# Low halves of queries and values on VectorE in the attention of a decoder step, and one weight half moved ahead of two key halves

## The chip, the cores and the metric

The kernel runs on one core of a Trainium2 chip. The metric is device time in microseconds (us) of one execution, as a median of runs. The core has TensorE (matmuls), VectorE and ScalarE (elementwise work and reductions, from and to PSUM as well), GpSimd (elementwise work from SBUF) and SyncE (SP), which here issues every DMA. The engines run side by side and wait for one another through semaphores; each does its own instructions in the order in which they are written.

## The reference, cut to what matters

One decoder layer for 1024 prompt tokens and 8 sample tokens, all in float32: a gated recurrence and a pooling mixer, then cross-attention over 256 memory tokens with 4 heads of 256, then a SwiGLU block. The part around the change is the cross-attention:

```python
def mem_kv(mem, g, w_kv):
    kv = rmsnorm(mem, g) @ w_kv
    k, v = jnp.split(kv, 2, axis=-1)
    ...

def cross_attend(h, mk, mv, w_q, w_o):
    q = (h @ w_q).reshape(B, L, X_HEADS, X_HEAD_DIM)
    s = jnp.einsum('blhd,bmhd->bhlm', q, mk) * (X_HEAD_DIM ** -0.5)
    p = jax.nn.softmax(s, axis=-1)
    o = jnp.einsum('bhlm,bmhd->blhd', p, mv)
    return o.reshape(B, L, D_MODEL) @ w_o
```

Keys and values of the memory (new_mem_k, new_mem_v) are outputs as well. The sample tokens attend to cached keys and values of their own, 8 samples with 256 memory tokens each.

## The kernel before

**Halves.** Every float32 product is made of three matmuls in the float32r format: an operand is split into a high half (rounded by ScalarE) and a low half (the operand minus its high half, one `tensor_tensor` subtraction), and hi x hi, lo x hi and hi x lo are added in PSUM. So each stripe of weights, and each block of queries, keys, values and softmax weights, costs a rounding on ScalarE and a subtraction on VectorE or GpSimd before TensorE may use it.

**Phases.** The phases run one after the other; the change lies in `kv` (keys and values of the memory) and in the attention behind it. In `kv` TensorE runs 8 key stripes and 8 value stripes, stripes 0 to 15; value stripe n is stripe 8 + n. Between them it computes the scores of the 8 samples (`sample_scores`), scores(0) and scores(1) of the prompt, and the first turn of softmax weights. The prompt's queries come in 8 blocks of 128 tokens (PAIRS = 8, numbered 0 to 7).

**TensorE's order** (the inner functions of `keys_values` and `attention` of the TensorE block): stripes 8, 9, sample 4, stripes 10, 11, sample 5, stripe 12, scores(0), stripe 13, sample 6, scores(1), turn_p(0), sample 7, stripe 14. Then for n = 1 to 7: scores(n + 1), turn_p(n) (transposes of block n's softmax weights), at n = 1 the last value stripe, from n = 3 on one or two `sample_values`, and from n = 2 on values(n - 2). scores(n) waits for the exponentials of n - 1 (they read the same PSUM banks) and for `qs_made`, the low half of query block n. turn_p(n) waits for `turned_rest(n - 1)`.

**Who makes what.** ScalarE: rounding of weight stripes (`w_hi`), of query blocks (`q_block`, tile `qs`, two buffers), of keys (`k_hi`), of values (`value_round`, tile `v_hi`), and four exponentials per block (`exps`). VectorE: the low halves of weight stripes (`split_low`, L1912), of keys (`key_rest`, L1935), the maximum (`maxima`, L1917), the normalisation (`normalize`, L1922 and L1924), the low half of turned weights (`turned_rest`, L1972), of outputs (`output_rest`, L1996), and the plain values (`value_kept`, L1966). GpSimd: the low halves of queries (`query_rest`, L928) and of values (`value_rest`, L936, in two halves of columns), masks, and the masked weights of the samples (L959).

**Stores that other work waits for.** The low half of the keys overwrites kT, so `key_rest` waits until the store of kT (L735) has landed; the low half of the values overwrites vnat, so `value_rest` waits for the store of that half of mem_v (L713).

**SP's order in `kv`.** For i = 3 to 7: loads of the two stripes 2i and 2i + 1 (each waits until the stripe whose buffer it takes has its low half), for i = 6 the store of kT (waits until all of kT is evacuated), then the cached keys of sample i - 1. Behind the loop come the keys of sample 7, the first mem_v store, loads of the next phase and of cached values, and the second mem_v store.

Of the kernel before, what the change touches and what calls it, by code (L numbers as in the profile page):

```python
# [29 lines left out]
F32 = mybir.dt.float32  # L30
# [4 lines left out]
P = 128  # L35
# [53 lines left out]
def hybrid_layer(nc, t):  # L89
# [9 lines left out]
    with ExitStack() as ctx:  # L99
# [421 lines left out]
        def _(sp):  # L521
            def load_stripe(p, i, s, wait=True):
                v, off, step, extra = stripe_src(p, i, s)
                if wait:

                    if p.name == "kv":
                        sp.wait_ge(lo_made, p.first + 2 * KV_FREE[i] + s + 1)
                    else:
                        sp.wait_ge(lo_made, p.first + 2 * i + s - 1)
                kb = v.shape[1]  # L530
                if p.name == "kv" and i >= KP:
                    dst, arrived, _ = raw_slot(p, i, s)
                    sp.dma_start(dst.rearrange("p (k a) c -> p k (a c)", k=2), v).then_inc(arrived, 16)
                    return
                src = v[:, :, bass.ds(i * step + (off + extra), P)]
                if p.name == "kv":
                    dst, arrived, _ = raw_slot(p, i, s)
                    sp.dma_start(dst, src).then_inc(arrived, 16)
                else:
                    sp.dma_start(raw[:, s, 0:kb, :], src).then_inc(raw_in[s], 16)  # L540
# [98 lines left out]
            for p in phases:  # L639
# [85 lines left out]
                if p.name == "kv":  # L725
                    sp.wait_ge(mem_step, 6)
                    sp.wait_ge(mem_sq, 2)
                    for s in range(2):
                        load_keys(1, s)
                    for i in range(3, p.stripes // 2):  # L730
                        for s in range(2):
                            load_stripe(p, i, s)
                        if i == 6:
                            sp.wait_ge(evac, p.done + KB)
                            sp.dma_start(t["mem_k_cols"], kT[:, :, :]).then_inc(kn_out, 16)  # L735
                        for s in range(2):
                            load_keys(i - 1, s)
                    for s in range(2):
                        load_keys(7, s)
# [60 lines left out]
        def _(pool):  # L800
# [124 lines left out]
            def query_rest(n):  # L925

                pool.wait_ge(q_round, QR + n + 1)
                pool.tensor_tensor(o_lo[:, :, n * P:(n + 1) * P], qT[:, :, n * P:(n + 1) * P], qs[n % 2][:, :, :].bitcast(F32),  # L928
                                   ALU.subtract).then_inc(qs_made, 1)

            def value_rest(c):

                pool.wait_ge(v_out, VO + 16 * (c + 1))
                pool.wait_ge(v_round, VR + 2 * (c + 1))
                at = slice(c * 512, (c + 1) * 512)
                pool.tensor_tensor(v_lo[:, :, at], vnat[:, :, at], v_hi[c][:, :, :].bitcast(F32), ALU.subtract).then_inc(v_rest, 1)  # L936

            def sample_values():

                for n in range(2):  # L940
                    query_rest(n)
                value_rest(0)
                for n in range(2, 4):
                    query_rest(n)
                pool.wait_ge(sk_done, NS + 1)
                pool.memset(smask[:, :, :], 0.0).then_inc(smask_made, 1)
                pool.wait_ge(smask_made, 1)
                for b in range(NS):
                    last = pool.memset(smask[:, b, b * H:(b + 1) * H], 1.0)
                last.then_inc(smask_made, 1)  # L950
                value_rest(1)
                query_rest(4)

                pool.wait_ge(ssm, 4)
                pool.wait_ge(smask_made, 2)
                for n in range(NS):
                    if n >= 2:
                        pool.wait_ge(sv_done, 2 * n - 2)
                    pool.tensor_tensor(spz[n % 2], spT[:, :, :], smask[:, n:n + 1, :].to_broadcast([P, 2, NS * H]),  # L959
                                       ALU.mult).then_inc(spz_made, 1)  # L960
                    if 1 <= n <= 3:
                        query_rest(n + 4)

            def squares(p, i, s, c):
                e = 6 * i + 3 * s + c
# [570 lines left out]
        def _(dve):  # L1536
# [369 lines left out]
            def split_low(m):  # L1906

                n = (p, m // 2, m % 2) if m < 16 else (ph["co"], 0, m - 16)
                count = n[0].first + 2 * n[1] + n[2]
                dve.wait_ge(lo_made, count)  # L1910
                dve.wait_ge(hi_made, count + 1)
                dve.tensor_tensor(w_lo[n[2]][:, :, :], raw_slot(*n)[0], w_hi[n[2]][:, :, :].bitcast(F32),  # L1912
                                  ALU.subtract).then_inc(lo_made, 1)
# [13 lines left out]
            def keys_values(p):  # L1927
                def turned_evac(j):
                    dve.wait_ge(mm_done, p.done + j + 1)
                    dve.tensor_tensor(kT[:, j, :], bank[4 + j % 2][:, 0:M], rbm[:, :], ALU.mult).then_inc(evac, 1)  # L1930

                def key_rest(n):
                    dve.wait_ge(kn_out, 16)
                    dve.wait_ge(k_round, KR + n + 1)
                    dve.scalar_tensor_tensor(k_lo[:, 4 * n:4 * n + 4, :], kT[:, 4 * n:4 * n + 4, :], -SCALE,  # L1935
                                             k_hi[:, 4 * n:4 * n + 4, :].bitcast(F32), ALU.mult,
                                             ALU.subtract).then_inc(k_rest, 1)

                split_low(1)
                for j in range(KB):  # L1940
                    turned_evac(j)
                    split_low(j + 2)
                split_low(10)
                key_rest(0)
                split_low(11)
                key_rest(1)
                split_low(12)
                value_kept(0, 0)
                value_kept(0, 1)
                split_low(13)  # L1950
                split_low(14)
                maxima(0)
                normalize(0)
                split_low(15)
                maxima(1)
                sample_maxima()
                normalize(1)
                sample_normalize()
                turned_rest(0)
                split_low(16)  # L1960

            def value_kept(c, a):
                dve.wait_ge(v_round, VR + 2 * c + a + 1)
# [11 lines left out]
            def sample_maxima():  # L1975
                dve.wait_ge(sk_done, NS + 1)
                dve.tensor_reduce(sst[:, 0:1], bank[7][:, 0:M], AX_X, ALU.min).then_inc(ssm, 1)
# [14 lines left out]
            def attention():  # L1992
                def output_rest(u):
                    dve.wait_ge(pv_hi, u + 1)
                    rows, at = slice(4 * (u % 2), 4 * (u % 2) + 4), slice(u // 2 * M, (u // 2 + 1) * M)
                    dve.tensor_tensor(o_lo[:, rows, at], wide(V_BANKS[u]).rearrange("p (k c) -> p k c", k=4),  # L1996
                                      o_hi[:, rows, at].bitcast(F32), ALU.subtract).then_inc(pv_out, 1)

                for n in range(1, PAIRS):
                    if n + 1 < PAIRS:  # L2000
                        maxima(n + 1)
                        normalize(n + 1)
                    if n == 2:
                        sample_turned()
                    turned_rest(n)
                    if n == 1:
                        value_kept(1, 0)
                        value_kept(1, 1)
                        split_low(17)
                    if n >= 2:  # L2010
                        output_rest(n - 2)
                output_rest(6)
                output_rest(7)

                dve.wait_ge(so_turned, 1)
                turned = [bank[6 + h // 2][:, 0:P].rearrange("p (k b h) -> p k b h", k=4, h=H)[:, 2 * (h % 2):2 * (h % 2) + 2, :, h]
                          for h in range(H)]
                for h in range(H):
                    last = dve.tensor_copy(o_hi[:, 2 * h:2 * h + 2, TP:T], turned[h])
                last.then_inc(so_made, 1)  # L2020
                dve.wait_ge(so_made, 1)
                for h in range(H):
                    last = dve.tensor_tensor(o_lo[:, 2 * h:2 * h + 2, TP:T], turned[h],
                                             o_hi[:, 2 * h:2 * h + 2, TP:T].bitcast(F32), ALU.subtract)
                last.then_inc(so_made, 1)
# [756 lines left out]
```

## Time and profile before

| what | value |
|---|---|
| median of 3 runs | 1440.44 us (1439.74 to 1442.37) |
| the profiled execution's own time | 1440.8 us |
| its span in the trace | 1439.1 us |
| mean granted TensorE clock | 0.994 of full speed |
| TensorE busy | 1409.3 us, 98% of the span |
| VectorE busy | 883.9 us, 61% |
| ScalarE busy | 420.3 us, 29% |
| GpSimd busy | 595.0 us, 41% |

All times of a row are microseconds from the start of the span. In the profile PE is TensorE, DVE is VectorE, ACT is ScalarE, POOL is GpSimd, and SPq is SP's queue of DMA issues. A busy share says how much an engine works, not whether somebody waits for it. So the reader goes from the engine table to the list of waits, and from there to the instructions in order of time around each wait: a row ends with the idle time ahead of it in brackets and the instruction that ended it. TensorE's matmul rows overlap by some 0.1 us, so the end of a group is best read from the start of the next.

### The profile page before, as it was taken

The page shows a single profiled execution, that of the slowest core. Times are in us where ns is not written, and L with a number is a line of the kernel's source. Part 1 is how long each engine was busy: PE and PEld are TensorE (multiplying, and loading weights), DVE is VectorE, ACT ScalarE, POOL GpSimd, SP SyncE. Part 2 cuts the span into 40 slices and gives each one's busy share as a digit, 9 for nine tenths or more (in the row PEclk, how much of TensorE's full clock was granted, in tenths as well). Part 3 has the DMA queues.
Part 4 walks back from the last instruction along what each step waited for, and adds up shares of the span by engine and source line. Part 5 has one row for each costly group of instructions (what it writes and reads, how often), then busy time and mean ns, then how long its engine had stood idle before and what let it go on. Part 6 is the DMA issues. An engine that isn't in the chain of part 4 may idle for free.

```text
span 1439.1 us, 25488 instructions
## 1 busy us (share of the span) xinstructions
PE 1409.3 (98%) x9965; PEld 1367.0 (95%) x9965; DVE 883.9 (61%) x1343; ACT 420.3 (29%) x632; POOL 595.0 (41%) x464
## 2 busy tenths in 40 slices
PE   8999999999999999899999999999999999999997
PEld 7999999989999977799999999999999999999996
DVE  4425677778753346557996666776677658632335
ACT  6131344471021135420052323232323223311111
POOL 1241246045532002424563877787777710000163
PEclk9999999999999999999999999999999999999998
DMA  9412111101161274511122222222222142523113
GB/s 294 125 44 79 54 30 38 38 23 59 44 190 44 87 259 140 184 63 45 44 74 79 84 88 73 71 75 88 73 80 66 59 143 85 169 89 113 34 44 118
DMA packets 163567, 129.19 MB, mean 90 GB/s; under 512 B 11532, under 2 KB 148748, under 8 KB 163363
## 3 DMA queue, kind: packets, MB, share of 16 engines
q1 hardware_dynamic: 163499, 128.25, 28.7%
q8 instruction: 47, 0.77, 0.2%
q14 instruction: 21, 0.17, 0.0%
HBM read 107.88 MB, written 20.58 MB: 89 GB/s over the span
## 4 chain that ended last, share of the span: by engine, by line
PE 62%; POOL 14%; issue 11%; DVE 7%; ACT 2%; DMA 1%; SPq 1%; POOLq 0%; DVEq 0%; ACTq 0%
PE pm L2235 17%; PE pm L2237 17%; PE pm L2236 17%; POOL gb L1003 3%; POOL raw_c L985 3%; POOL raw L985 3%; POOL sum L992 2%; POOL sum L990 2%; PE pm L2506 1%; PE pm L2508 1%; PE pm L2507 1%; DMA xt<-in_x_prompt 1%; POOL raw L997 1%; POOL raw_c L997 1%; DVE w_lo L1549 1%
## 5 line engine op out<-in xcount | busy, mean ns | idle before, releaser
L2235 PE MATMUL pm<-x_hi,w_hi 128*128 128x344 f32 x960 | 310.5, 323 | 0.7 <-DVE gb L1616 0.7
L2237 PE MATMUL pm<-x_hi,w_lo 128*128 128x344 f32 x960 | 306.6, 319 | 0.0
L2236 PE MATMUL pm<-x_lo,w_hi 128*128 128x344 f32 x960 | 306.6, 319 | 0.0
L1088 ACT ACTIVATE w_hi<-raw 128x1024 fp32r<-128x1024 f32 x88 | 93.4, 1061 | 530.3 <-PE pm L2237 465.4
L2235 PEld LDWEIGHTS pm<-x_hi,w_hi 128*128 128x128 f32 x960 | 180.4, 188 | 2.6 <-issue 1.9
L2236 PEld LDWEIGHTS pm<-x_lo,w_hi 128*128 128x128 f32 x960 | 180.4, 188 | 0.2
L2237 PEld LDWEIGHTS pm<-x_hi,w_lo 128*128 128x128 f32 x960 | 180.4, 188 | 0.0
L1549 DVE TENSOR_TENSOR w_lo<-raw,w_hi 128x1024 fp32r<-128x1024 f32 x79 | 113.8, 1440 | 10.0 <-ACT w_hi L1088 10.0
L831 POOL TENSOR_TENSOR raw<-raw,gains 128x1024 f32<-128x1024 f32 x32 | 64.7, 2026 | 127.3 <-DMA raw<-in_w_in 81.1
L2082 DVE TENSOR_TENSOR gb<-gb,ga 128x1032 f32<-128x1032 f32 x19 | 53.0, 2788 | 89.9 <-POOL gb L1003 89.9
L913 POOL TENSOR_TENSOR fp<-acc 128x344 f32 (+1 forms) x22 | 21.3, 969 | 201.8 <-DVE acc L2193 196.9
L2193 DVE TENSOR_TENSOR acc<-pm,acc 128x344 f32<-128x344 f32 x66 | 33.9, 516 | 112.1 <-PE pm L2237 112.0
L1002 POOL TENSOR_TENSOR ga<-ga,rb 128x1032 f32<-128x1032 f32 x19 | 52.6, 2768 | 85.9 <-DVE ga L2098 85.9
L2506 PE MATMUL pm<-x_hi,w_hi 128*128 128x258 f32 x304 | 86.5, 285 | 0.2
L2507 PE MATMUL pm<-tl,wh 128*128 128x258 f32 x304 | 85.9, 283 | 0.0
L2506 PE MATMUL pm<-th,wh 128*128 128x258 f32 x304 | 85.9, 282 | 0.0
L2508 PE MATMUL pm<-th,wl 128*128 128x258 f32 x304 | 85.9, 282 | 0.0
L2507 PE MATMUL pm<-tl,w_hi 128*128 128x258 f32 x304 | 85.8, 282 | 0.0
L2508 PE MATMUL pm<-x_hi,w_lo 128*128 128x258 f32 x304 | 85.8, 282 | 0.0
L2508 PE MATMUL pm<-th,w_lo 128*128 128x258 f32 x304 | 85.7, 282 | 0.0
L2507 PE MATMUL pm<-x_lo,w_hi 128*128 128x258 f32 x304 | 85.7, 282 | 0.0
L2506 PE MATMUL pm<-th,w_hi 128*128 128x258 f32 x304 | 85.7, 282 | 0.0
(364 smaller groups left out, 3996.2 us busy)
## 6 DMA issues: line engine op xcount, KB each, us to landing
raw<-in_w_ffn_in SPq DMA_DIRECT2D x24, 512.0 KB, 4.5
sg_raw<-s_rows SPq DMA_DIRECT2D x22, 516.0 KB, 5.1
s_rows<-gb SPq DMA_DIRECT2D x21, 516.0 KB, 2.7
raw<-in_w_in SPq DMA_DIRECT2D x20, 512.0 KB, 3.8
raw_c<-in_w_ffn_in SPq DMA_DIRECT2D x20, 512.0 KB, 5.0
sk<-in_cache_k_cols SPq DMA_DIRECT2D x16, 512.0 KB, 6.4
raw<-in_w_out SPq DMA_DIRECT2D x8, 512.0 KB, 3.6
raw<-in_w_cq SPq DMA_DIRECT2D x8, 512.0 KB, 3.5
```

Source lines behind the costliest of these rows:

```text
L831: pool.tensor_tensor(raw[:, s, :, :], raw[:, s, :, :], g, ALU.mult).then_inc(gain_on, 1)
L985: pool.tensor_tensor(r[:, s, :, :], r[:, s, :, :], g, ALU.mult).then_inc(gain7_on, 1)
L1002: pool.tensor_tensor(ga[:, :], ga[:, :], rb[:, :], ALU.mult).then_inc(row_scaled, 1)
L1088: act.activation(w_hi[s][:, :, :], src, ACT.Copy).then_inc(hi_made, 1)
L1549: dve.tensor_tensor(w_lo[s][:, :, :], raw[:, s, :, :], w_hi[s][:, :, :].bitcast(F32), ALU.subtract).then_inc(lo_made, 1)
L2082: dve.tensor_tensor(gb[par][:, :], gb[par][:, :], ga[:, :], ALU.mult).then_inc(row_made, 1)
L2235: pe.matmul(out, w_hi[s][:, k, :], hi[:, k, x0:x0 + cols], start=(k == 0), stop=False)
L2236: pe.matmul(out, w_hi[s][:, k, :], lo[:, k, x0:x0 + cols], start=False, stop=False)
L2237: last = pe.matmul(out, w_lo[s][:, k, :], hi[:, k, x0:x0 + cols], start=False, stop=(k == kb - 1))
L2506: pe.matmul(out, wh7[n][:, j, :], hi(j, c), start=j == 0, stop=False)
L2507: pe.matmul(out, wh7[n][:, j, :], lo(j, c), start=False, stop=False)
L2508: last = pe.matmul(out, wl7[n][:, j, :], hi(j, c), start=False, stop=j == KP - 1)
```

## The change

- VectorE gets `query_rest` and `value_rest`. The low halves of query blocks 2 to 7 and of the first half of the values are made there; GpSimd keeps those of blocks 0 and 1 and of the second half of the values, which also waits for the first.
- In VectorE's queue query_rest(n) stands between a maximum and the normalisation behind it: block 2 between maxima(0) and normalize(0), 3 between maxima(1) and normalize(1), and 4 to 7 between maxima and normalize of blocks 3 to 6. value_rest(0) stands behind split_low(15) and ahead of maxima(1).
- split_low(11) goes ahead of key_rest(0) and split_low(12) ahead of key_rest(1).
- In SP's queue the store of kT goes ahead of the loads of stripes 12 and 13.

```diff
@@ SP, phase kv
                     for i in range(3, p.stripes // 2):
-                        for s in range(2):
-                            load_stripe(p, i, s)
                         if i == 6:
                             sp.wait_ge(evac, p.done + KB)
                             sp.dma_start(t["mem_k_cols"], kT[:, :, :]).then_inc(kn_out, 16)
+                        for s in range(2):
+                            load_stripe(p, i, s)
                         for s in range(2):
                             load_keys(i - 1, s)
@@ GpSimd
                 pool.wait_ge(v_round, VR + 2 * (c + 1))
+                pool.wait_ge(v_rest, VL + 1)
@@ GpSimd, sample_values
                 for n in range(2):
-                    query_rest(n)
-                value_rest(0)
-                for n in range(2, 4):
                     query_rest(n)
@@
                 value_rest(1)
-                query_rest(4)
@@
-                    if 1 <= n <= 3:
-                        query_rest(n + 4)
@@ VectorE, keys_values
                 split_low(10)
+                split_low(11)
                 key_rest(0)
-                split_low(11)
+                split_low(12)
                 key_rest(1)
-                split_low(12)
                 value_kept(0, 0)
                 value_kept(0, 1)
                 split_low(13)
                 split_low(14)
                 maxima(0)
+                query_rest(2)
                 normalize(0)
                 split_low(15)
+                value_rest(0)
                 maxima(1)
                 sample_maxima()
+                query_rest(3)
                 normalize(1)
@@ VectorE, new functions
+            def query_rest(n):
+                dve.wait_ge(q_round, QR + n + 1)
+                dve.wait_ge(qs_made, n)
+                dve.tensor_tensor(o_lo[:, :, n * P:(n + 1) * P], qT[:, :, n * P:(n + 1) * P], qs[n % 2][:, :, :].bitcast(F32),
+                                  ALU.subtract).then_inc(qs_made, 1)
+
+            def value_rest(c):
+                dve.wait_ge(v_out, VO + 16 * (c + 1))
+                dve.wait_ge(v_round, VR + 2 * (c + 1))
+                at = slice(c * 512, (c + 1) * 512)
+                dve.tensor_tensor(v_lo[:, :, at], vnat[:, :, at], v_hi[c][:, :, :].bitcast(F32), ALU.subtract).then_inc(v_rest, 1)
@@ VectorE, attention
                     if n + 1 < PAIRS:
                         maxima(n + 1)
+                        if n >= 2 and n + 2 < PAIRS:
+                            query_rest(n + 2)
                         normalize(n + 1)
```

## Rows read from the trace of the kernel before

**Rows 1.** The page's engine table: busy us, share of the span, instructions.
```profile
PE 1409.3 (98%) x9965; PEld 1367.0 (95%) x9965; DVE 883.9 (61%) x1343; ACT 420.3 (29%) x632; POOL 595.0 (41%) x464
```

**Rows 2.** TensorE's waits, whole span: us in total, times, longest us.
```profile
PE pm L2549 <- POOL o_lo L928: 6.1, 1, 6.1
...
PE pm L2608 <- DVE w_lo L1912: 2.5, 1, 2.5
PE pm L2549 <- ACT pr L1321: 1.7, 2, 1.5
```

**Rows 3.** Stretches: length, busy PE PEld DVE ACT POOL, granted clock, DMA share, GB/s.
```profile
534.00:536.00 2.00, 0.09 (x1) 0.00 (x0) 1.86 (x2) 1.06 (x1) 0.00 (x0) 1.00 0.96 381
538.00:539.00 1.00, 1.00 (x4) 0.73 (x3) 0.77 (x1) 0.25 (x1) 0.00 (x0) 0.50 0.51 137
580.00:581.00 1.00, 0.00 (x0) 0.00 (x0) 1.00 (x2) 0.00 (x0) 1.00 (x1) 0.50 0.00 0
620.00:700.00 80.00, 80.00 (x533) 79.75 (x532) 57.43 (x90) 10.52 (x11) 33.13 (x36) 1.00 0.16 47
```

**Rows 4.** TensorE in order of time: start, us, instruction, idle before.
```profile
536.56 0.50 PE L2608 MATMUL pm<-w_hi,m_hi 128*128 128x512 f32 x1 [2.47 <-DVE w_lo L1912]
...
561.12 0.36 PE L2549 MATMUL pm<-k_hi,qs 128*128 128x256 f32 x1 [1.47 <-ACT pr L1321]
564.19 1.06 PE L2560 MATMUL pm<-ident,pr 128*128 128x128 f32 x8
...
581.52 0.58 PE L2549 MATMUL pm<-k_hi,qs 128*128 128x256 f32 x1 [6.08 <-POOL o_lo L928]
```

**Rows 5.** The chain that ended last, in order of time: start, us, what.
```profile
530.14 0.98 PE pm L2574 x16
...
541.16 0.98 PE pm L2574 x16
...
586.29 0.87 PE pm L2560 x8
```

**Rows 6.** VectorE from 534 us on, in order of time.
```profile
534.14 1.22 DVE L1935 SCALAR_TENSOR_TENSOR k_lo<-kT,k_hi 128x1024 fp32r<-128x1024 f32 x1 [4.23 <-DMA out_mem_k_cols<-kT]
535.28 1.22 DVE L1912 TENSOR_TENSOR w_lo<-raw,w_hi 128x1024 fp32r<-128x1024 f32 x1
```

**Rows 7.** SP's queue: the kT store.
```profile
526.43 0.47 SPq L735 DMA_DIRECT2D out_mem_k_cols<-kT  x1
```

**Rows 8.** DMA issues at 526.4, 527.4, 543.0 and 572.2: KB, us to landing.
```profile
out_mem_k_cols<-kT SPq DMA_DIRECT2D x1, 1024.0 KB, 7.7
...
sk<-in_cache_k_cols SPq DMA_DIRECT2D x1, 512.0 KB, 9.2
...
out_mem_v<-vnat SPq DMA_DIRECT2D x1, 512.0 KB, 8.0
...
out_mem_v<-vnat SPq DMA_DIRECT2D x1, 512.0 KB, 3.5
```

**Rows 9.** GpSimd in order of time, 551 to 582 us.
```profile
553.43 6.70 POOL L928 TENSOR_TENSOR o_lo<-qT,qs 128x1024 fp32r<-128x1024 f32 x2
...
575.83 2.35 POOL L936 TENSOR_TENSOR v_lo<-vnat,v_hi 128x1024 fp32r<-128x1024 f32 x1 [15.07 <-DMA out_mem_v<-vnat]
578.13 3.34 POOL L928 TENSOR_TENSOR o_lo<-qT,qs 128x1024 fp32r<-128x1024 f32 x1
```

**Rows 10.** VectorE in the attention, in order of time.
```profile
576.70 0.18 DVE L1922 RECIPROCAL rden<-den 128x4 f32<-128x4 f32 x1 [2.00 <-ACT pr L1321]
576.92 2.33 DVE L1924 TENSOR_TENSOR pr<-pr,rden 128x1024 f32<-128x1024 f32 x1
...
594.09 1.23 DVE L1917 TENSOR_REDUCE nmax<-pm 128x4 f32<-128x1024 f32 x1 [0.57 <-PE pm L2551]
...
602.73 1.22 DVE L1917 TENSOR_REDUCE nmax<-pm 128x4 f32<-128x1024 f32 x1 [0.57 <-PE pm L2551]
```

**Rows 11.** ScalarE: the last query rounding.
```profile
600.80 1.06 ACT L1314 ACTIVATE qs<-qT 128x1024 fp32r<-128x1024 f32 x1
```

## The prediction, made before the changed kernel was run

> **What bounds the kernel now.** I read the engine table first, then TensorE's waits, then the stretches. TensorE is busy 98% of the span and no other engine passes 61% [rows 1]: what the kernel can gain is what TensorE stands idle, plus what it runs at the lower clock. The table of TensorE's waits says where it stands [rows 2]: 6.1 us for the queries' low halves of GpSimd (one wait), 2.5 us for a weight half of VectorE (one wait), 1.7 us in two waits for the exponentials. All lie between 534 and 582 us, where keys and values end and the attention begins. Behind the attention the stretch from 620 to 700 us has 80.00 busy us of 80.00 [rows 3], so what is won ahead of it is kept.
>
> The clock is the second loss. The granted clock is 0.50 (1.2 GHz) in the samples behind the 2.5 us wait and behind the 6.1 us wait [rows 3]; before both it was 1.00. In durations: a value stripe takes 531.12 to 534.09, 2.97 us, and the one behind the first wait 536.56 to 541.16, 4.60 us: 1.6 us lost. The scores of a pair take 561.12 to 564.19, 3.07 us, and those behind the second wait 581.52 to 586.29, 4.77 us: 1.7 us lost [rows 4, 5]. The wait of 1.47 us at 561.12 was followed by full speed (the same 3.07 us).
>
> So the pot is 2.5 + 1.6 + 1.5 + 0.2 + 6.1 + 1.7 = 13.6 us of a profiled run of 1440.8 us.
>
> **Part 1: SP's order and the order of three VectorE instructions.** Value stripe 3 (stripe 11) starts at 536.56, when its low half, made 535.28 to 536.50, is there. That half stood in VectorE's queue behind k_lo (L1935), which had waited 4.23 us for the store of kT to land and began at 534.14 [rows 4, 6]. Now split_low(11) stands ahead of key_rest(0). ScalarE rounds it when stripe 9 is done, at 530.1 [rows 5], in 1.06 us (a row of the same size) [rows 11], so it can be made by about 532.5, ahead of 534.09 where TensorE wants it. The 2.5 us wait goes, and the clock's 1.6 us with it. No instruction is added.
>
> What is late next: key_rest(0), then split_low(12). TensorE wants stripe 12's low half at 538.0 (stripe 3 and one sample product of 0.98 us later), and ScalarE rounds it at 534.2 to 535.2 in either order, so split_low(12) ends at 536.5 if key_rest(0) has begun by 534.0. It needs the kT store. SP issued this at 526.43, right behind stripe 13's load [rows 7]; now it goes as soon as kT is whole, about 524.0, and by the 7.7 us of its row [rows 8] it lands at 531.7; it would have to be 2.3 us later to cost anything. The two raw_b loads are moved behind it: stripe 12's by about 1.4 us (at the 7.7 us of the store it lands at 532.2, wanted at 534.1), stripe 13's not at all, since it waited for a VectorE half until 526.0. Cost: nothing, from the slack of 2 us; if that is gone, the wait comes back a stripe later.
>
> The keys of sample 5 follow, and TensorE now wants them 4.1 us earlier. Their second half landed 9.2 us after its issue at about 527.4, so at 536.6 [rows 8]; the sample product is now due at 537.1. Same bytes ahead of them, so the same landing: 0 us, with 0.5 us of slack only. Bounds: 0 and 1.5 us, since the DMA engines are 0.96 busy from 534 to 536 [rows 3] and can't catch up. I take 0.
>
> **Part 2: the low halves on VectorE.** Removed from GpSimd: six query_rest and one value_rest. They took 2.4 to 3.4 us each: two in 6.70 us at 553.43, one of 3.34 us at 578.13 [rows 9]. Added to VectorE: seven tensor_tensor of the same 128x1024 size. Beside an idle GpSimd VectorE does such an instruction in 1.22 us (the halves at 534.14 and 535.28) [rows 6]. That is 8.5 us more on an engine with gaps.
>
> Where they lie: between maxima(n) and normalize(n) VectorE waits 2.00 us for ScalarE's four exponentials, in every step (576.70 is one of seven such rows; the wait at 561.00 is 1.67) [rows 10]. One instruction of 1.14 to 1.22 us fits, if its rounded query is there. The last of them was made at 600.80 to 601.86, and the maximum in whose shadow it is now used began at 602.73 [rows 10, 11]: there ahead of time. Cost: 0; uncovered it would be 6 x 1.2 = 7.3 us.
>
> What goes: (a) GpSimd's chain. At 575.83 it began v_lo of the second half (it had waited 15.07 us, in the end for the mem_v store), with query 4's low half behind it, which ended at 581.47: TensorE's 6.1 us [rows 9]. Now that half is in VectorE's queue, at about 569. (b) Mutual blocking. The 1.22 us normalisation took 2.33 at 576.92, ending 1.07 us after GpSimd's v_lo ended at 578.18, and GpSimd's row behind it took 3.34 where others took 2.4 [rows 9, 10]. It stretched VectorE's work behind 551 us, beside GpSimd's 6.70 us, in the same way. Without it maxima(1) isn't late, and the 1.5 us wait of scores(2) goes.
>
> What is late next. With every wait gone TensorE would be ready for scores(4) at 581.5 - 2.5 - 1.6 - 1.5 - 0.2 - 6.1 = 569.6. It then needs exponentials 3. Before, these ended at 576.6, when TensorE had been free since 575.44: 1.2 us that the GpSimd wait covered [rows 5, 10]. VectorE is now less behind at maxima(2) (0.3 instead of 0.9 us), so I take 0.7 us; bounds 0 and 1.4.
>
> One GpSimd instruction of size is left: v_lo of the second half. Its store took 3.5 us [rows 8]. It goes when both vnat halves are written, when SP issued it at 572.2 [rows 8]; TensorE's stripe 7 ahead of them comes 2.5 + 1.6 + 1.5 = 5.6 us earlier, ScalarE's exponentials 2 another 0.6: 566.0. So GpSimd works 569.6 to 572.0. normalize(3), due at 570.5, is held to 572.0, as the row of 2.33 us shows [rows 10], and ends at 573.1; sample_turned (0.3) and turned_rest(2) (1.2) let turn_p(3) start at 574.5. TensorE, with scores(4) from 570.3, is done at 573.4: 1.1 us (bounds 0 and 2.0, the second if v_lo starts 1 us later).
>
> The Trainium skill (Perfetto Trace Analysis, Optimizing Scalar/DVE Operations) speaks against this part: the two engines share an SBUF read port, so offloading between them "might not help". The rows do show the blocking, but also 1.22 us for the work on one engine and 2.4 on the other; by the skill's rule the sum would be that of rival 2.
>
> **An added wait.** value_rest(0) stands in VectorE's queue for the first mem_v store, and behind it maxima(1), exponentials 1 and scores(2). The store took 8.0 us [rows 8]. It is now issued at about 539.1 (4 us earlier), so it lands at 547.1. VectorE reaches it at 549.8 and maxima(1) is due at 550.6: 0 us; it would cost from a landing after 551.2 on (exponentials 1 have that slack).
>
> **Sum.** 13.6 us, minus 0.7, minus 1.1: 11.8 us. From the profiled run's 1440.8 us this gives 1429.0; the median of the runs shown, 1440.44, is 0.4 us lower, so the forecast is 1428.6.
>
> **Rivals.**
> 1. *A transfer takes the wait's place.* Keys 5 late, or the kT store landing after 534, or the mem_v store after 551.2. For it: DMA share 0.96 around 535 [rows 3]. Against: each has slack by the rows. Price: one wait of about 2.5 us with its low clock, 2.5 + 1.6 = 4.1, leaves a gain of 7.7: 1432.7, and up to 1434. Chance 0.14.
> 2. *The move buys nothing*: the port is held by VectorE instead, the exponentials and halves keep TensorE waiting as long as GpSimd did. Then only part 1 (4.1 us) stays: 1436.3. Against: GpSimd's 3.34 us instructions become 1.22 us. Chance 0.04.
> 3. *Part 1 does not do what it says* (the half of stripe 11 is late for another reason, its load), part 2 works: 11.8 - 4.1 = 7.7, again 1432.7. Chance 0.04.
> 4. *Slower: VectorE becomes the bound of the attention.* A step on it is the maximum (1.2), 2.0 us of exponentials with the new instruction inside, and three more of 1.22 with a reciprocal (3.9): 7.1 us, against 8.6 us from maximum to maximum as TensorE sets them now (594.09 to 602.73) [rows 10]. It decides when the step passes 8.6: not with one blocked instruction, but if the remaining GpSimd products held both two-input instructions of a step for 3.3 us, as VectorE held GpSimd's at 578.13 [rows 9]. Then a step is 1.2 + 3.3 + 3.3 + 2.4 + 0.2 = 10.4 us; five steps lose 1.8 each and, with a gap in each, 1.7 of clock: 17.5 us, less the 11.8: 1446.1. Against: VectorE still waits for TensorE before each maximum from 594 on (0.57 us at 594.09 and 602.73) [rows 10]. Chance 0.03.
>
> **How the numbers follow.** The forecast has 0.75. Its own range: all bounds good, 13.6 us gained, 1426.8; all bad (0.7 + 0.9 + 1.5 more lost), 1431.7. To hold 8 in 10 I reach into rivals 1 and 3: 1426.0 to 1433.5. A measurement of this kernel tells 0.2%, 2.9 us. Faster by more: 0.75 + 0.14 + 0.04 + 0.04 less a little of each that is worse than priced: 0.94. Within: 0.03. Slower: 0.03.
>
> **What would show it.** Right: no TensorE wait at L2608 and stripe 3 next to stripe 2; clock 1.00 from 530 to 620; scores(4) starts near 570 us after a wait under 1.5 us on exponentials; query halves of 1.2 us inside the 2 us of the exponentials; one GpSimd v_lo with a stretched normalisation beside it. Wrong: a new wait of TensorE on sample keys (L2574) or on L1935, VectorE idle before value_rest(0), or low clock anywhere in the stretch.

## The result, and the profile after

| | before | after |
|---|---|---|
| median of the runs side by side | 1441.35 us (4 runs) | 1429.83 us (4 runs) |
| profiled execution's own time | 1440.8 us | 1430.4 us |
| its span | 1439.1 us | 1428.7 us |
| mean granted TensorE clock | 0.994 | 0.997 |

The ratio of the times is 0.9928, with a 95% interval of 0.9915 to 0.994: 0.7% faster, which is 10.4 us (8.6 to 12.3). The two medians of the table differ by 11.5 us; the ratio and its interval are what the document goes by. The forecast was 1428.6 us, 11.8 us less than the 1440.44 known then, in a range of 1426.0 to 1433.5.

TensorE's waits after, in the same view as [rows 2] (us in total, times, longest). Of the three rows of before, the GpSimd one (6.1 us) and the weight half (2.5 us) are gone; a wait for exponentials of 1.4 us is left, a new one of 0.9 us stands at turn_p, and one of 0.5 us at the keys of a sample.

```profile
PE pm L2561 <- ACT pr L1316: 1.4, 1, 1.4
...
PE pm L2572 <- DVE o_lo L1982: 0.9, 1, 0.9
...
PE pm L2586 <- DMA sk<-in_cache_k_cols: 0.5, 1, 0.5
```

The stretches after, as in [rows 3]: the granted clock is 1.00 over the whole attention, and the stretch behind it is as full as before.

```profile
530.00:620.00 90.00, 87.06 (x672) 72.21 (x671) 63.61 (x66) 48.06 (x101) 6.96 (x18) 1.00 0.55 189
...
620.00:700.00 80.00, 80.00 (x515) 79.75 (x515) 63.23 (x99) 7.43 (x7) 40.64 (x42) 1.00 0.13 39
```

VectorE after, in order of time, the same view as [rows 6, 10]. The reader is to see the half of stripe 11 at 532.43, ahead of the key half; the value half at 550.88 with no idle time ahead of it; and the query half of 1.21 us at 569.66 between the maximum and the reciprocal, which now waits 0.87 us for the exponentials where it waited 2.00.

```profile
532.43 1.23 DVE L1907 TENSOR_TENSOR w_lo<-raw,w_hi 128x1024 fp32r<-128x1024 f32 x1 [1.49 <-ACT w_hi L1083]
533.57 1.22 DVE L1930 SCALAR_TENSOR_TENSOR k_lo<-kT,k_hi 128x1024 fp32r<-128x1024 f32 x1
...
550.88 1.22 DVE L1970 TENSOR_TENSOR v_lo<-vnat,v_hi 128x1024 fp32r<-128x1024 f32 x1
552.02 1.22 DVE L1912 TENSOR_REDUCE nmax<-pm 128x4 f32<-128x1024 f32 x1
...
567.39 1.22 DVE L1907 TENSOR_TENSOR w_lo<-raw,w_hi 128x1024 fp32r<-128x1024 f32 x1
568.53 1.22 DVE L1912 TENSOR_REDUCE nmax<-pm 128x4 f32<-128x1024 f32 x1
569.66 1.21 DVE L1963 TENSOR_TENSOR o_lo<-qT,qs 128x1024 fp32r<-128x1024 f32 x1
571.75 0.18 DVE L1917 RECIPROCAL rden<-den 128x4 f32<-128x4 f32 x1 [0.87 <-ACT pr L1316]
571.96 2.40 DVE L1919 TENSOR_TENSOR pr<-pr,rden 128x1024 f32<-128x1024 f32 x1
```

The normalisation at 571.96 takes 2.40 us. GpSimd's row beside it, the one large instruction left there (compare [rows 9]), ran until 573.28:

```profile
570.90 2.38 POOL L937 TENSOR_TENSOR v_lo<-vnat,v_hi 128x1024 fp32r<-128x1024 f32 x1 [16.37 <-DMA out_mem_v<-vnat]
```

TensorE's two waits in order of time, as in [rows 4]: scores(4) at 571.86 (before 581.52), and turn_p(3) held by turned_rest(2) behind that normalisation.

```profile
571.86 0.35 PE L2561 MATMUL pm<-k_hi,qs 128*128 128x256 f32 x1 [1.40 <-ACT pr L1316]
...
575.84 1.07 PE L2572 MATMUL pm<-ident,pr 128*128 128x128 f32 x8 [0.91 <-DVE o_lo L1982]
```

The sum of the two traces closes. scores(4) starts 9.7 us earlier (581.52 to 571.86); its 24 matmuls take 3.1 us instead of 4.8, another 1.7; the new wait of 0.9 us is given back: 10.5 us, against 10.4 of the spans. But this is the sum of a larger gain and a loss. In a part that the change does not touch, at the spreading of the first norm factors, TensorE waited 0.22 us for ScalarE before and 1.44 us after:

```profile
35.70 0.90 PE L2255 MATMUL pm<-ident,rtok 128*128 128x128 f32 x6 [0.22 <-ACT rtok L1123]
```

```profile
36.76 0.90 PE L2267 MATMUL pm<-ident,rtok 128*128 128x128 f32 x6 [1.44 <-ACT rtok L1118]
```

So everything up to stripe 10 comes 1.0 us later: the product of sample 4 starts at 530.1 before and at 531.1 after. From there to turn_p(3) TensorE took 56.2 us before (to 586.3) and 44.7 after (to 575.8): the stretch that was changed is 11.5 us shorter.

### The profile page after: what moved, and what is told of

It is laid out like the page before. It is cut to its first block, busy times and chain, and to the rows that moved or that the text cites. A ratio compares the mean times of both kernels' runs of the same rounds, so it can differ in the third digit from the quotient of the medians.

```text
span 1428.7 us, 25494 instructions
## 1 busy us (share of the span) xinstructions
PE 1404.9 (98%) x9965; PEld 1364.1 (95%) x9965; DVE 886.8 (62%) x1350; ACT 420.3 (29%) x632; POOL 577.5 (40%) x457
## 4 chain that ended last, share of the span: by engine, by line
PE 65%; POOL 12%; issue 10%; DVE 7%; ACT 2%; DMA 2%; SPq 1%; POOLq 0%; DVEq 0%; ACTq 0%
PE pm L2247 17%; PE pm L2249 17%; PE pm L2248 17%; POOL gb L998 2%; POOL raw_c L980 2%; POOL raw L980 2%; PE pm L2518 2%; PE pm L2520 2%; PE pm L2519 2%; POOL sum L987 2%; POOL sum L985 2%; DMA xt<-in_x_prompt 1%; DMA sk<-in_cache_k_cols 1%; DVE w_lo L1544 1%; POOL raw L992 1%
```

## The experiments

The question: do the two parts of the change do what the prediction says, and do they add up? The rivals: the place in a queue and not the engine; the place of the store and not that of the halves; a pot that either part empties; and VectorE being full. There are twelve runs.

**The order alone** (SP's and VectorE's order changed; all low halves stay on GpSimd).

```diff
--- before
+++ this
@@ SP
-                        for s in range(2):
-                            load_stripe(p, i, s)
                         if i == 6:
...
+                        for s in range(2):
+                            load_stripe(p, i, s)
@@ VectorE
                 split_low(10)
+                split_low(11)
                 key_rest(0)
-                split_low(11)
+                split_low(12)
                 key_rest(1)
-                split_low(12)
```

> Only the order is changed (SP's kT store ahead of the loads of stripes 12 and 13, split_low(11) and split_low(12) one place ahead); the low halves stay on GpSimd. My theory: the two parts of the change add up, and this one is worth the 2.5 us wait of value stripe 3 and the 1.6 us of low clock behind it: 4.1 us, 1437 us. The waits of 1.5 us (scores of block 2) and 6.1 us (scores of block 4) and the low clock behind the latter stay. Rival 'one pot': what is won here is given back at the attention, because GpSimd's mem_v store sets its own time: then the 6.1 us wait grows to about 10 us and the time stays near 1441.

Measured: ratio 0.9965 [0.9953, 0.9976], 5.0 us faster; in its profile the wait and the low clock at stripe 3 are gone, and the attention is that of before, the 6.2 us wait included. The span is 4.3 us shorter than before's. The theory stands: nothing is given back.

```profile
PE pm L2549 <- POOL o_lo L928: 6.2, 1, 6.2
```

**The halves alone, twice** (the second time profiled beside before).

```diff
--- the change
+++ this (low halves as in the change, order as before)
@@ SP
+                        for s in range(2):
+                            load_stripe(p, i, s)
                         if i == 6:
...
-                        for s in range(2):
-                            load_stripe(p, i, s)
@@ VectorE
                 split_low(10)
-                split_low(11)
                 key_rest(0)
+                split_low(11)
-                split_low(12)
                 key_rest(1)
+                split_low(12)
```

> Only the low halves are moved to VectorE; SP's order and the order of the weight and key halves are those of before. My theory: 1.5 + 0.2 + 6.1 + 1.7 us go, 1.4 (exponentials of block 3) and 0.9 us (turn_p(3)) stay: 7.2 us won, 1434 us; the 2.5 us wait of stripe 3 and its low clock stay. Rival 'one pot': with stripe 3 late the chain behind it has more slack, and the whole 11 us minus less than 2 come from this part: 1431.

> The low halves alone on VectorE, the order as before, profiled once more beside before. Theory 'it varies with the landing': 1430.5 us again, a wait of stripe 3 anywhere from 0.5 to 2.5 us and equal to the landing of the kT store less about 5.2 us. Rival 'in this kernel the wait is short': 1.4 us again and no low clock, while before shows 2.5 us beside it.

> The kernel before itself, profiled once more. Open: the wait of value stripe 3 was 2.47 us with a low clock behind it in the first profile of before, and 1.39 us with none in the run of the halves alone, whose instructions up to there are the same. Theory 'it varies with the landing': the kT store lands 5 to 8 us after its issue from run to run, and the wait is that landing less about 5.2 us; the clock falls only when the wait is over 2 us. Then this run shows 0.5 to 2.5 us. Rival 'the first profile is typical': 2.4 to 2.5 us and 1.6 us of low clock again. The 6.1 us wait is there in either case: 1439 to 1441 us.

Measured: the halves alone have ratio 0.9929 [0.9913, 0.9946], and 0.994 [0.9922, 0.9958] the second time: 10.2 and 8.6 us faster, where 7.2 was expected. 1430.77 us is what the rival 'one pot' had named for the first, but not by its mechanism: the waits at scores(4) and turn_p(3) are those of the whole change, and no slack took them up. The whole change in its two sets of runs isn't clearly more, 0.9928 and 0.9926. The waits left in their profiles account for it: 13.6 - 1.4 - 1.4 - 0.9 = 9.9 us, and 13.6 - 2.5 - 1.4 - 1.1 = 8.6, if no clock is lost at stripe 3. So the parts don't add (5.0 + 9.4 = 14.4 against 10.5). Of the 3.9 us between, 1.6 are clock at stripe 3, which the order alone wins and the halves alone don't lose, up to 1.1 are the shorter wait in the first profile of the halves alone, and 0.5 the wait for keys in the profile of the change; the rest is within the intervals. TensorE at stripe 3 shows the first two. The rows of before again, of the halves alone and of the halves alone again:

```profile
537.89 0.66 PE L2608 MATMUL pm<-w_hi,m_hi 128*128 128x512 f32 x1 [2.09 <-DVE w_lo L1912]
```

```profile
535.03 0.50 PE L2620 MATMUL pm<-w_hi,m_hi 128*128 128x512 f32 x1 [1.39 <-DVE w_lo L1907]
```

```profile
536.24 0.50 PE L2620 MATMUL pm<-w_hi,m_hi 128*128 128x512 f32 x1 [2.48 <-DVE w_lo L1907]
```

The wait was 2.47 [rows 4] and 2.09 us in the two profiles of before and 1.39 and 2.48 us in the two of the halves alone. It follows the landing of the kT store, which came 7.7, 7.3, 6.6 and 7.7 us after its issue. Less 5.2 these are 2.5, 2.1, 1.4 and 2.5: that half of the theory holds. The other half, that the clock falls only behind a longer wait, falls: behind 2.09 us it fell, behind 2.48 us it didn't. First before again, then the halves alone again, the microseconds behind the wait (columns as in [rows 3]):

```profile
540.00:541.00 1.00, 1.00 (x4) 0.75 (x3) 0.10 (x1) 0.28 (x1) 0.00 (x0) 0.50 0.72 172
```

```profile
538.00:539.00 1.00, 1.00 (x6) 0.72 (x4) 0.74 (x2) 0.62 (x1) 0.00 (x0) 1.00 0.92 190
```

Both profiles of before had the 1.6 us of low clock at stripe 3, and both of the halves alone had not. Up to there the two kernels issue the same instructions, so I can't name a cause in the kernel, and two against two may be chance. This is left open; the time it decides is 1.6 us.

**The whole change without SP's move, and without VectorE's reordering.**

```diff
--- the change
+++ without SP's move
@@ SP
+                        for s in range(2):
+                            load_stripe(p, i, s)
                         if i == 6:
...
-                        for s in range(2):
-                            load_stripe(p, i, s)
--- the change
+++ without the reordering
@@ VectorE
-                split_low(11)
                 key_rest(0)
+                split_low(11)
-                split_low(12)
                 key_rest(1)
+                split_low(12)
```

> The whole change without SP's part: the kT store is issued behind the loads of stripes 12 and 13, as before. My theory: the order on VectorE alone is enough. The store lands at about 535 instead of 532.9, the first key half is made behind it and stripe 12's half by 537.6, due at 539: no wait, 1430 us, as the whole change. Rival 'the store's place carries it': stripe 12 now waits where stripe 3 waited, 2 us and a low clock, 1433.5 us.

> The whole change without VectorE's part of the order: split_low(11) stands behind key_rest(0) as before, the kT store is still moved ahead on SP. My theory: the store lands at 532.9, the key half takes until 534.1, stripe 11's half until 535.3, and TensorE wants it at 535.1: a wait of 0.3 us with no low clock behind it, 1430 us. Rival 'only the queue order matters': the wait is 1.5 us or more and the clock falls, 1433 us.

Measured: 1429.59 us, ratio 0.9923 [0.9906, 0.9939], and 1431.02 us, ratio 0.9932 [0.9909, 0.9954]. Neither has a wait at stripe 3 or stripe 12. Without SP's move the key half waits 1.17 us for the store, at 533.31, and harms nobody, since both weight halves come in time. Without the reordering the store landed early, 5.3 us after its issue at 524.96, and the key half at 530.80 was done before stripe 11's rounded half was there:

```profile
530.80 1.22 DVE L1930 SCALAR_TENSOR_TENSOR k_lo<-kT,k_hi 128x1024 fp32r<-128x1024 f32 x1
532.37 1.23 DVE L1907 TENSOR_TENSOR w_lo<-raw,w_hi 128x1024 fp32r<-128x1024 f32 x1 [0.35 <-ACT w_hi L1083]
```

In these runs either half of part 1 was enough, and neither rival ("the store's place carries it", "only the queue order matters") came. The second wasn't put to a hard test: at the 7.9 us of the change's own store a short wait was expected, and no run shows that case. The same store landed 5.1 to 7.9 us after its issue in all kernels but the one with three more edits below, so the order on VectorE is the sturdier of the two: it doesn't depend on a landing.

**All low halves on GpSimd, one swap in its queue.**

```diff
--- the order alone
+++ this
@@ GpSimd
-                value_rest(1)
                 query_rest(4)
+                value_rest(1)
```

> The order part of the change, and all low halves still on GpSimd, with one swap in its queue: query block 4's half ahead of the second v_lo (before: behind it). My theory: most of the 6.1 us wait came from that place in the queue. Scores of block 4 then wait only for the exponentials (1 to 2 us), the clock doesn't fall; the 1.5 us wait at scores(2) stays, since that comes from GpSimd and VectorE blocking each other. Won: 4.1 + 4.5 + 1.7 = about 10, less 1 to 2 us for blocked VectorE instructions: 1432 us. Rival 'the engine matters': GpSimd's 2.4 to 3.4 us instructions keep block 4 or the next blocks late, and it gives no more than the order alone, 1437 us.

Measured: 1432.07 us, ratio 0.9947 [0.9929, 0.9965], 7.6 us faster by the ratio; 1432 was expected. The 6.1 us wait for GpSimd is gone with the low halves still there: it came from the place of query 4 behind v_lo in GpSimd's queue. What is left is what the two engines do to each other. Its VectorE and GpSimd rows:

```profile
548.48 3.42 DVE L1912 TENSOR_TENSOR w_lo<-raw,w_hi 128x1024 fp32r<-128x1024 f32 x1
...
555.24 2.33 DVE L1924 TENSOR_TENSOR pr<-pr,rden 128x1024 f32<-128x1024 f32 x1
...
567.48 2.50 DVE L1912 TENSOR_TENSOR w_lo<-raw,w_hi 128x1024 fp32r<-128x1024 f32 x1
```

```profile
566.51 2.39 POOL L928 TENSOR_TENSOR o_lo<-qT,qs 128x1024 fp32r<-128x1024 f32 x1 [9.38 <-ACT qs L1314]
```

Three VectorE instructions of 1.22 us take 2.3 to 3.4. TensorE waits 1.1 us at turn_p(1), where a wait of 1.5 us at scores(2) was expected. At scores(4) it waits 2.7 us for exponentials whose maximum stood behind the 2.50 us one; the granted clock was 0.50 from 575 to 577, and this run of scores took 4.2 us instead of 3.1.

```profile
573.23 0.36 PE L2549 MATMUL pm<-k_hi,qs 128*128 128x256 f32 x1 [2.67 <-ACT pr L1321]
```

These rows lose 5.1 us (2.7 + 1.1 + 1.1 of clock + 0.2 at scores(3)), those of the change 2.3 to 2.8. So by the rows the move to VectorE is worth some 2 to 3 us beyond a mere reordering; the intervals of the two ratios, 0.9929 to 0.9965 and 0.9915 to 0.994, still overlap.

**The last large GpSimd instruction on VectorE.**

```diff
--- the change
+++ this
@@ GpSimd
-                value_rest(1)
@@ VectorE, attention
                     turned_rest(n)
+                    if n == 2:
+                        value_rest(1)
```

> The whole change, and the second half of the values' low half also on VectorE, behind turned_rest(2); GpSimd has no large instruction left. My theory: the normalisation of block 3 takes 1.22 instead of 2.40 us, turn_p(3) doesn't wait (0.9 us won), and the maximum of block 4 comes at the same time as before, since 1.2 us less blocking pays for 1.2 us more work: 1429 us. Rival 'VectorE is full': the maximum of block 4 is later and scores(5) waits for its exponentials, 1430 us or more.

Measured: 1428.04 us, ratio 0.992 [0.9902, 0.9938]. The normalisation of block 3 takes 1.23 us, the wait at turn_p(3) is gone, and no wait stands at scores(5). The maximum of block 4 starts 1.8 us after scores(4) ends in either kernel (575.21 and 573.44; in the change 576.75 and 574.93). As expected: VectorE isn't full.

**The weight half of the next phase behind the maximum.**

```diff
--- the change
+++ this
@@ VectorE, attention
                         maxima(n + 1)
+                        if n == 2:
+                            split_low(17)
...
                         value_kept(1, 1)
-                        split_low(17)
```

> The whole change, and split_low(17), the low half of a weight stripe that TensorE wants only after the attention, moved from ahead of the maximum of block 3 to behind it. My theory: the wait of scores(4) for the exponentials falls from 1.4 to about 0.3 us, but the normalisation of block 3 is still held by GpSimd's v_lo, so turn_p(3) starts at the same time and waits about 2.0 us instead of 0.9: nothing won, 1430 us. Rival 'the waits add': 1.1 us won, 1428.7 us.

> The changed kernel with split_low(17) behind the maximum of block 3, again and in more rounds: 1426.3 us, 2.3 us under the changed kernel (1428.7 to 1429.8). The normalisation of block 3 starts 0.1 us ahead of GpSimd's v_lo, which then waits for it. If that order is a matter of luck, this run shows the normalisation held for 1 us and a wait of turn_p(3) instead, and 1427.3 us.

Measured: 1426.2 us, ratio 0.9909 [0.9891, 0.9926], and 1429.19 us, ratio 0.9909 [0.9889, 0.9929], where the runs of before beside it were slower as well. My theory of no gain fell, and the rival was too small. The wait at scores(4) fell from 1.40 to 0.21 us as expected (it is now for the query's low half), but the one at turn_p(3) went as well. VectorE, then GpSimd, of the first of the two runs:

```profile
568.72 0.17 DVE L1917 RECIPROCAL rden<-den 128x4 f32<-128x4 f32 x1
568.93 1.22 DVE L1919 TENSOR_TENSOR pr<-pr,rden 128x1024 f32<-128x1024 f32 x1
```

```profile
569.05 3.38 POOL L937 TENSOR_TENSOR v_lo<-vnat,v_hi 128x1024 fp32r<-128x1024 f32 x1 [16.36 <-DMA out_mem_v<-vnat]
```

The normalisation started 0.12 us ahead of v_lo, took 1.22 us, and GpSimd took 3.38 instead of 2.38. In the change it started 1.06 us behind (571.96 and 570.90) and VectorE lost instead. In the repeated run the gap was 0.06 us (573.17 and 573.23), with the same outcome. This agrees with the Trainium skill (SBUF — State Buffer, Who interferes with whom): a VectorE instruction with two SBUF inputs contends with a GpSimd instruction that reads SBUF, and the order of issue decides which of them blocks. The 1 us is paid in either case; on GpSimd nobody waits for it.

**All three remaining waits at once, beside the change again.**

```diff
--- the change
+++ this (with both edits above as well)
@@ SP
-                        if i == 6:
-                            sp.wait_ge(evac, p.done + KB)
-                            sp.dma_start(t["mem_k_cols"], kT[:, :, :]).then_inc(kn_out, 16)
                         for s in range(2):
                             load_stripe(p, i, s)
                         for s in range(2):
                             load_keys(i - 1, s)
+                        if i == 6:
+                            sp.wait_ge(evac, p.done + KB)
+                            sp.dma_start(t["mem_k_cols"], kT[:, :, :]).then_inc(kn_out, 16)
@@ VectorE
                 split_low(11)
-                key_rest(0)
                 split_low(12)
+                key_rest(0)
                 key_rest(1)
```

> The whole change with three more edits: the second v_lo on VectorE, split_low(17) behind the maximum of block 3, and the keys of sample 5 ahead of the kT store in SP's queue with both key halves behind split_low(12). My theory: the waits left in the stretch (0.46 us for the keys of sample 5, 1.4 us at scores(4), 0.9 us at turn_p(3)) all go, with 0.2 us left at scores(5): 2.5 us won against the changed kernel beside it, 1427.3 us if that is 1429.8. Rival 'VectorE is full': the waits reappear at scores(5) or at scores(0), and less than 1 us is won.

> The changed kernel itself again, beside the run above on the same chip: 1429.8 us, waits of 0.46, 1.4 and 0.9 us in the stretch from 530 to 580 us.

Measured: 1426.93 us, ratio 0.9909 [0.9894, 0.9924], beside 1428.65 us, ratio 0.9926 [0.9913, 0.9939], of the change. So 1.7 us were won against the 2.5 expected. The kT store, now last, was issued at 527.5 and landed at 537.8, 10.3 us later; both key halves and the values behind them came late, and scores(0) waited 0.8 us. That is a place which the rival named, but for the store and not because VectorE is full:

```profile
537.85 2.36 DVE L1929 SCALAR_TENSOR_TENSOR k_lo<-kT,k_hi 128x1024 fp32r<-128x1024 f32 x2 [1.17 <-DMA out_mem_k_cols<-kT]
540.12 1.40 DVE L1975 TENSOR_SCALAR vnat<-pm,rtok 128x512 f32<-128x512 f32 x2
```

The change, profiled again, showed 1.40 and 0.90 us, nearly as in its first profile, but no wait for sample 5's keys, and no other profile has it: the 0.46 us is a matter of one run's landing, and the third edit mends nothing. The best ratio seen is 0.9909, twice with split_low(17) alone moved and once with all three edits, against 0.9928 and 0.9926 for the change. The intervals overlap, so the last 2 us or so rest on the profiles (1.40 to 0.21 and 0.91 to none) as much as on the times.

## Why the prediction was right, point by point

- **What bounds.** Right. TensorE's waits and the clock were the whole pot, and behind the attention nothing was given back (80.00 of 80.00 us from 620 to 700 both times).
- **Part 1, 4.1 us.** Right against before: the wait is gone in the profile, and the order alone measured 5.0. Stripe 12 and its load were in time. As a term of a sum it isn't shown: on top of part 2 the order brought about 1 us (10.5 against 9.4), which the intervals don't tell from nothing. That a single one of the two moves can suffice I had not said. The 1.6 us of clock in the term isn't tied to the wait alone: the halves alone kept a 2.48 us wait at full speed.
- **Keys of sample 5.** I took 0 us with bounds of 0 and 1.5. The trace has 0.46 us, and 0 in the change profiled again: the slack of 0.5 us was used up in one run. There the second half of the keys was issued at 528.66 and took 9.5 us, not 9.2.
- **Part 2, the wait of 6.1 us and the 1.5 us at scores(2).** Both gone, with the clock's 1.7. Of the two mechanisms named, the queue place (a) was the larger: GpSimd reordered has no wait for GpSimd either. The blocking (b) stretches the rows as said, but that the 1.5 us of scores(2) come from it alone isn't shown: with GpSimd reordered three rows are still stretched, and there the wait is 1.1 us at turn_p(1) and none at scores(2).
- **The added instructions cost nothing.** Right: 1.21 us each while VectorE waited for exponentials anyway, which left 0.87 of 2.00 us of idle time (none in block 1's step, where the sample's maximum stands there too); value_rest(0) found its store landed (no idle time ahead of 550.88), 7.4 us after its issue at 540.26.
- **Exponentials 3, 0.7 us.** Too small: 1.40, at my upper bound. The step that failed is "VectorE is now less behind at maxima(2) (0.3 instead of 0.9 us)". Measured from the start of scores(2), that maximum came 3.62 us later (556.52 to 560.14), against 3.97 before (561.12 to 565.09): only 0.35 us less. From maxima(2) to maxima(3) VectorE took 8.4 us in both. And TensorE's own way from scores(2) to the end of values(0) was 13.94 us, against 14.32 before with a wait of 0.2 in it, which gave 0.38 us away again. The 1.2 us that the estimate began with was too small as well. After, scores(4) starts 0.11 us behind the reciprocal (571.86 and 571.75); before, that would have been at 576.81, 1.37 us behind 575.44. So 1.37 - 0.35 + 0.38 = 1.40.

```profile
565.09 1.22 DVE L1917 TENSOR_REDUCE nmax<-pm 128x4 f32<-128x1024 f32 x1
```

```profile
560.14 1.22 DVE L1912 TENSOR_REDUCE nmax<-pm 128x4 f32<-128x1024 f32 x1
```

- **turn_p(3), 1.1 us.** Measured 0.91, by the mechanism named: the normalisation was held until GpSimd's v_lo ended at 573.28 and ended 1.08 us behind it (before: 1.07). It can be had for nothing by coming first, which I hadn't seen.
- **The sum.** By the waits that are left it is 13.6 - 1.4 - 0.9 - 0.5 = 10.8 us, where I had 11.8; the difference is the exponentials (0.7) and the keys (0.5), less 0.2 at turn_p(3). That 10.4 was measured is in part luck: the changed stretch won 11.5 us, 0.7 more than these terms say, and 1.0 us was lost ahead of it. The pot was counted too small. The idle time in a row isn't all that a wait costs, since rows overlap when there is none: from the start of scores(2) to that of the next instruction it was 3.07 us behind the wait before (561.12 to 564.19) and 2.84 without one after (556.52 to 559.36). Not all of the 0.7 us is placed by this. The change profiled again, with neither the wait ahead nor the one for the keys, has a span of 1426.7 us, 12.4 less than before's first profile.
- **Rivals.** A transfer in the wait's place: 0.46 us of it came, with no low clock. The move buys nothing: as priced, refuted by the halves alone (8.6 and 10.2 us), though that has the better queue place in it; the engine by itself is worth the 2 to 3 us above. The Trainium skill's caution (Perfetto Trace Analysis, Optimizing Scalar/DVE Operations) is that offloading between the two might not help; here the work took 1.22 us on VectorE instead of 2.4 to 3.4 on GpSimd, and by the rows the move helped. VectorE as the bound: it had 0.57 us of idle time before the maximum at 592.44, as in before.

## What to carry to other kernels

A wait for an engine that is 41% busy is first a question of order: read what stands ahead of the wanted instruction in its queue, and what that one waits for (here a store's landing). Where an engine has a fixed idle time in each step, as VectorE has for the exponentials, an instruction that another engine does more slowly fits in at no cost. The cheapest edit here was such a swap: with the order of part 1 it brought 7.6 of the 10.4 us. And when two savings may share a wait or a clock fall, measure each alone and both together: here the parts alone were 5.0 and 9.4 us, both together 10.5.

## What the runs showed of the hardware that I had not expected

- A wait of 2.48 us of TensorE was followed by a granted clock of 1.00 (2.4 GHz), waits of 2.09, 2.47 and 2.67 us by 0.50 (1.2 GHz). The length of a wait alone doesn't tell whether the clock falls.
- VectorE and GpSimd with two SBUF inputs each took turns in whole instructions: behind, VectorE's normalisation took 2.40 us instead of 1.22; ahead by 0.12 and 0.06 us, it took 1.22 and GpSimd's v_lo 3.4 instead of 2.4. VectorE's subtraction from PSUM (o_lo from pm) kept its 1.21 us beside GpSimd's 3.34 us row at 578.13 of [rows 9].
- The same 1 MB store landed 5.1 to 7.9 us after its issue in runs of nearly the same kernel, and 10.3 us after it where it stood behind the loads and the keys. A term that hangs on one landing needs that spread as its bounds.
- A wait of 3.0 us at the start of the output projection (for y_lo) stood in the second profile of before and in the repeated run with split_low(17) moved, 0.4 us in the first profile of before. It lies ahead of the change; it is why one run's time says less than its rows.
